# Both feed-forward networks of a hybrid encoder layer in two stages, with seven block products in place of eight for gate and up

## The chip, the core and the metric

The kernel runs on one core of one Trainium2 chip. The metric is the device time of one execution in microseconds (us), lower is better. The core's engines are TensorE (PE; its weight loads are PEld in the profile), VectorE (DVE), ScalarE (ACT), GpSimd (POOL) and SyncE (SP, which issues the DMAs).

## What is computed

One layer of an encoder over 1024 tokens of width 1024, all in float32. It opens and closes with a SwiGLU feed-forward network (FFN) of inner width 2816. Between the two stand a projection, attention, a state-space mixer and a merge, which the change does not touch.

```python
SEQ = D_MODEL = 1024
D_FF = 2816
def _swiglu(x, w_gate, w_up, w_down):
    return (jax.nn.silu(x @ w_gate) * (x @ w_up)) @ w_down
...
        h = h + FFN_RES * _swiglu(_rmsnorm(h, ffn1_norm[l]), ffn1_w_gate[l], ffn1_w_up[l], ffn1_w_down[l])
...
        h = h + FFN_RES * _swiglu(_rmsnorm(h, ffn2_norm[l]), ffn2_w_gate[l], ffn2_w_up[l], ffn2_w_down[l])
    return _rmsnorm(h, final_norm)
```

## The kernel before

`build` runs the phases one after the other with a barrier between them; `ffn_phase` stands first ("f1", rows loaded from x) and last ("f2", with the final norm, class `Finish`). The residual stream lies in SBUF as `rows`, 8 token tiles of 128 x 1024.

**Precision.** Each float32 product is made of three: every operand is split into a high part (ACT rounds it to fp32r, L528) and a low part (DVE or POOL subtracts, L532), and `three_passes` (L46 to L50) issues high x high, high x low and low x high into one PSUM bank. Each matmul has a 128 x 128 stationary and a 128 x 512 moving operand.

**Head.** `Norm` squares the rows (ACT, L283), takes roots, scales (DVE, L325), and PE turns each token tile (8 transposes, L364) into PSUM; ACT and DVE (L339) write it back as `nT_hi` and `nT_lo`. PE starts the first gate product for the first 512 tokens once six of the eight tiles have been turned, and turns the last two between products. POOL splits the low parts of the first four weight tiles (L532).

**Body.** The 2816 inner columns are 11 pairs of 128-wide tiles. For a pair p, `gate_up(p)` makes four products (two tiles, gate and up), each for two halves of the tokens: 8 inner blocks x 3 passes x 2 halves, 192 matmuls in all. ACT applies Silu (L550), DVE multiplies by up (L598), and ACT and DVE split the result into `hT_hi` (L562) and `hT_lo` (L601). `down(q)`, for the pair before, multiplies it by two 128 x 1024 tiles of w_down: 8 token tiles x 2 halves x 2 inner tiles x 3 passes, 96 matmuls. PSUM has eight banks and they are shared: gate, up and down take turns, so after each token tile DVE adds half of the two banks into `rows` (L584, `add`), and the next `gate_up` waits for the last of these adds (`added`). Weights come in pieces of 512 KB through three raw buffers. PE, ACT, DVE and SP loop over pairs, with two pairs in a body (four in number) on PE.

**End.** The last two `down` calls stand back to back. In "f2" the DVE queue mixes the last adds with the scaling of the output rows (L415), and SP stores them.

## Time and profile before

| | us |
|---|---|
| device time, median of 3 runs (2611.12 to 2617.19) | 2611.46 |
| the profiled execution, device time | 2620.58 |
| its span, first to last instruction | 2618.8 |
| PE busy in that span | 2355.1 (90%) |
| DVE / ACT / POOL busy | 1138.8 / 674.0 / 133.8 |
| "f1" and "f2" together | about 60% of the span |

The page cuts the span into 40 slices of 65.5 us. The first 11.8 slices are "f1", the last 12 are "f2"; PE is busy in over 90% of nearly all of them. The profiled execution's own time is 0.35% above the median. PE's busy time is no measure of its rate, since matmuls overlap: the distance between the starts of two of them is.

### The profile page before, as it was taken

To read this page: it belongs to the slowest core of one execution; us is meant where nothing else is said; L and a number is where in the kernel's file an instruction comes from. 1 tells how busy PE (TensorE), PEld (TensorE's weight loads), DVE (VectorE), ACT (ScalarE), POOL (GpSimd) and SP (SyncE) were. 2 spreads that over 40 slices of the span, in tenths; PEclk is the share of its full clock that TensorE was granted. 3 is DMA by queue.
4 is the path that set the end of the run, shared out by engine and by line. 5 is a ranking of instruction groups with operands and counts; after the bars stand their busy time and mean duration, and the time that the engine had idled before them with its cause. 6 is when DMAs were issued, how large, how long until landed. Compare 5 with 4: busy or idle time off the path is not lost. (4 is left out here: it accounts for less than half of the span.)

```text
span 2618.8 us, 27137 instructions
## 1 busy us (share of the span) xinstructions
PE 2355.1 (90%) x10898; PEld 1951.9 (75%) x10898; DVE 1138.8 (43%) x1493; ACT 674.0 (26%) x964; POOL 133.8 (5%) x97
## 2 busy tenths in 40 slices
PE   6999999999978896795968998799799999999997
PEld 5888888888867886685846776577688888888885
DVE  4333333333245294697337777442433333333325
ACT  4211111111112321314226667320321111111112
POOL 1000000000000010220002222000100000000000
PEclk8999999999998998898989999799899999999998
DMA  3211111111012322221240000241221111111101
GB/s 128 81 49 44 45 48 48 48 48 48 16 43 77 88 70 45 57 89 41 81 129 6 6 6 1 86 171 34 71 75 49 49 48 48 42 47 48 48 25 64
DMA packets 174039, 146.96 MB, mean 56 GB/s; under 512 B 27968, under 2 KB 154176, under 8 KB 173952
## 3 DMA queue, kind: packets, MB, share of 16 engines
q1 hardware_dynamic: 173952, 145.77, 18.6%
q8 instruction: 59, 0.97, 0.2%
q14 instruction: 28, 0.23, 0.0%
HBM read 120.58 MB, written 23.07 MB: 55 GB/s over the span
## 5 line engine op out<-in xcount | busy, mean ns | idle before, releaser
L48 PE MATMUL psum<-f_nT_hi,f_w_hi 128*128 128x512 f32 x1408 | 551.7, 392 | 23.9 <-DVE rows L584 23.9
L49 PE MATMUL psum<-f_nT_lo,f_w_hi 128*128 128x512 f32 x1408 | 549.2, 390 | 0.0
L50 PE MATMUL psum<-f_nT_hi,f_w_lo 128*128 128x512 f32 x1408 | 548.7, 390 | 0.0
L48 PEld LDWEIGHTS psum<-f_nT_hi,f_w_hi 128*128 128x128 f32 x1408 | 265.0, 188 | 86.1 <-DVE rows L584 27.8
L584 DVE SCALAR_TENSOR_TENSOR rows<-psum,rows 128x1024 f32<-128x1024 f32 x176 | 215.4, 1224 | 221.2 <-PE psum L50 221.2
L50 PEld LDWEIGHTS psum<-f_nT_hi,f_w_lo 128*128 128x128 f32 x1408 | 264.9, 188 | 55.6
L49 PEld LDWEIGHTS psum<-f_nT_lo,f_w_hi 128*128 128x128 f32 x1408 | 265.0, 188 | 54.4
L48 PE MATMUL psum<-f_d_hi,f_hT_hi 128*128 128x512 f32 x704 | 275.3, 391 | 7.3 <-issue 7.3
L49 PE MATMUL psum<-f_d_lo,f_hT_hi 128*128 128x512 f32 x704 | 275.2, 391 | 0.0
L50 PE MATMUL psum<-f_d_hi,f_hT_lo 128*128 128x512 f32 x704 | 275.1, 391 | 0.0
L532 DVE TENSOR_TENSOR f_w_lo<-f_raw,f_w_hi 128x1024 fp32r<-128x1024 f32 x80 | 97.6, 1220 | 398.3 <-ACT f_w_hi L528 398.3
L598 DVE TENSOR_TENSOR f_xn<-psum,f_xn 128x1024 f32<-128x1024 f32 x44 | 53.9, 1225 | 359.7 <-PE psum L50 359.7
L528 ACT CAST f_w_hi<-f_raw 128x1024 fp32r<-128x1024 f32 x88 | 92.2, 1048 | 333.6 <-PE psum L50 333.6
L48 PEld LDWEIGHTS psum<-f_d_hi,f_hT_hi 128*128 128x128 f32 x704 | 132.8, 189 | 35.8 <-issue 8.0
L50 PEld LDWEIGHTS psum<-f_d_hi,f_hT_lo 128*128 128x128 f32 x704 | 133.0, 189 | 27.7
L49 PEld LDWEIGHTS psum<-f_d_lo,f_hT_hi 128*128 128x128 f32 x704 | 132.9, 189 | 27.8
L550 ACT ACTIVATE f_xn<-psum 128x1024 f32<-128x1024 f32 x44 | 45.2, 1028 | 408.3 <-PE psum L50 408.3
L528 ACT CAST f_d_hi<-f_raw 128x1024 fp32r<-128x1024 f32 x44 | 43.9, 1044 | 388.6 <-PE psum L50 388.6
L1728 DVE TENSOR_TENSOR at_PT_lo<-psum,at_PT_hi 128x512 fp32r<-128x512 f32 x128 | 87.7, 686 | 71.8 <-ACT at_PT_hi L1624 71.5
L48 PE MATMUL psum<-nT_hi,g_hi 128*128 128x512 f32 x256 | 101.8, 398 | 7.2 <-POOL g_lo L164 7.2
L49 PE MATMUL psum<-nT_lo,g_hi 128*128 128x512 f32 x256 | 101.0, 395 | 0.0
L50 PE MATMUL psum<-nT_hi,g_lo 128*128 128x512 f32 x256 | 100.9, 394 | 0.0
(282 smaller groups left out, 3284.6 us busy)
## 6 DMA issues: line engine op xcount, KB each, us to landing
f_raw<-ffn_w_gate SPq DMA_DIRECT2D x44, 512.0 KB, 4.7
f_raw<-ffn_w_up SPq DMA_DIRECT2D x44, 512.0 KB, 3.9
f_raw<-ffn_w_down SPq DMA_DIRECT2D x44, 512.0 KB, 3.5
g_raw<-w_in SPq DMA_DIRECT2D x16, 512.0 KB, 4.7
gates<-rows SPq DMA_DIRECT2D x10, 512.0 KB, 3.0
rows<-x SPq DMA_DIRECT2D x8, 512.0 KB, 7.2
kept<-rows SPq DMA_DIRECT2D x1, 4096.0 KB, 12.9
gl_gate<-gates SPq DMA_DIRECT2D x8, 512.0 KB, 4.6
```

What stands on the lines that cost most here:

```text
L48: pe.matmul(out, lhs_hi, rhs_hi, start=first, stop=False)
L49: pe.matmul(out, lhs_hi, rhs_lo, start=False, stop=False)
L50: return pe.matmul(out, lhs_lo, rhs_hi, start=False, stop=last)
L528: act.copy(dst, raw[slot][:]).then_inc(w_hi_done, 1)
L532: dve.tensor_tensor(dst, raw[slot][:], hi.bitcast(F32), ALU.subtract).then_inc(w_lo_done, 1)
L550: act.activation(two(h[:, t, :]), ps2(2 * t), ACT.Silu).then_inc(silu_done, 1)
L584: dve.scalar_tensor_tensor(out=two(rows[:, m, :]), in0=ps2(m % 4), scalar=0.5, in1=two(rows[:, m, :]), op0=ALU.mult, op1=ALU.add).then_inc ...
L598: dve.tensor_tensor(two(h[:, t, :]), ps2(2 * t + 1), two(h[:, t, :]), ALU.mult).then_inc(mult_done, 1)
L1728: dve.tensor_tensor(pt(PT_lo, g, x), turned_bank(x), pt(PT_hi, g, x).bitcast(F32), ALU.subtract).then_inc(s["tr_lo"], 1)
```

## The change

`ffn_phase` is written anew, for both FFNs. The other phases stay.

**Stage one, gate and up.** For each pair of inner tiles the weight block (1024 x 256) is seen as 2 x 2 blocks A of 512 x 128, and the normed activations (1024 x 1024, turned) as 2 x 2 blocks B of 512 x 512. The product's four quarters come from seven block products in place of eight (Winograd's form of Strassen's scheme), each of 4 inner blocks x 3 passes = 12 matmuls of the same shape as before. Four combinations of B (`T`) are made once in the head by POOL (`combine`), for four pairs of token tiles; PE turns seven 128 x 512 blocks for each pair (`turn`), and ACT and DVE keep the high and low parts of all seven (`B_hi`, `B_lo`). Four combinations of A (`S`) are made by POOL for each of the 22 matrices (11 pairs, gate and up; `sums`). Of a matrix PE makes products q = 0 to 6 into three banks; ACT copies the first (`t1`), and DVE adds `t1`, `t2`, `t3` to the others as they end, which gives the quarters of gate or up in the space of `rows`. The operands of matrix n+1 are split, product by product, while matrix n runs. Silu and gate x up follow, and the hidden activations of the pair go to a DRAM tensor, `hidden`.

**Stage two, down.** All 22 tiles of w_down (512 KB each) are loaded into the space of B as the last matrix frees it. A unit is one inner tile for one half of the tokens: 4 token tiles x 2 halves x 3 passes = 24 matmuls, into all eight banks, which hold the sum over the whole depth of 22 units. There are 44 units; their hidden tiles (256 KB) come back from DRAM through eight buffers. `rows` is loaded again, from x or, in "f2", from a copy in DRAM that is stored in the head. DVE adds a token tile once, at the end of its half. The last adds and the final norm then have their own order.

PE loops over pairs (ten iterations of 168 matmuls) and over units (nine iterations of 48 matmuls for each half); ACT, DVE, POOL and SP are written out without loops.

The diff, cut to its core:

```diff
...
+PAIRS = F // (2 * P)
+MATS = 2 * PAIRS
+FT = F // P
+QUAD = ST // 2
+KH = KT // 2
+PRODUCTS = 7
+GATE_BANKS, UP_BANKS = (7, 0, 1), (2, 3, 4)
+QUARTER = {(0, 0): 0, (1, 1): 1, (1, 0): 2, (0, 1): 3}
...
+        B_hi, B_lo = (at(n, [P, PRODUCTS, KH, HALF], F32R, n) for n in ("B_hi", "B_lo"))
+        A_hi, A_lo = (at(n, [P, PRODUCTS, KH, P], F32R, n) for n in ("A_hi", "A_lo"))
+        raw = [at(f"raw{j}", [P, KT, 2 * P], F32, "raw", 8 * KB * j) for j in range(2)]
...
+        T = at("T", [P, 4, HALF], F32, "raw", 8 * KB)
+        wd_raw = [at(f"wd_raw{k}", [P, D], F32, ("B_hi", "B_lo")[k % 4 // 2], 8 * KB * (k // 4) + 4 * KB * (k % 2)) for k in range(FT)]
+        h_raw = [at(f"h_raw{u}", [P, HALF], F32, "raw", 8 * KB * (u % 2) + 2 * KB * (u // 2)) for u in range(8)]
...
+            load_matrix(0)
+            if x is None:
+                sp.dma_start(residual.rearrange("(m p) d -> p m d", p=P), rows[:]).then_inc(s_kept, 16)
+            sp.wait_ge(s_tr, PRODUCTS * QUAD)
+            load_matrix(1)
+            for p in range(PAIRS):
                 for j in range(2):
...
+                    n = 2 * p + j
+                    if n + 2 < MATS:
+                        sp.wait_ge(s_lo, PRODUCTS * (n + 1))
+                        load_matrix(n + 2)
+                    if j == 0 and p:
+                        sp.wait_ge(s_h, p)
+                        sp.dma_start(hidden[p - 1].rearrange("q f s -> f q s"), h).then_inc(s_hout, 16)
+            def load_unit(u):
+                sh, k = u // FT, u % FT
+                sp.dma_start(h_raw[u % 8][:], hidden[k // 2, QUARTER[k % 2, sh]]).then_inc(s_hraw[u % 8], 16)
+            sp.wait_ge(s_hout, 16 * (PAIRS - 1))
+            sp.wait_ge(s_lo, PRODUCTS * MATS)
+            for u in range(8):
+                load_unit(u)
+            for k in range(FT):
+                if k % 4 == 0:
+                    sp.wait_ge(s_mm, PRODUCTS * (MATS - 1) + k // 4 + 1)
+                sp.dma_start(wd_raw[k][:], w_down[k * P:(k + 1) * P, :]).then_inc(s_wd[k // 4], 16)
+            sp.wait_ge(s_h, PAIRS)
+            sp.dma_start(hidden[PAIRS - 1].rearrange("q f s -> f q s"), h).then_inc(s_hout, 16)
+            sp.wait_ge(s_hout, 16 * PAIRS)
+            sp.wait_ge(s_c12, MATS)
+            for m in range(ST):
+                sp.dma_start(rows[:, m, :], residual[m * P:(m + 1) * P, :]).then_inc(s_res, 16)
...
+            for u in range(8, UNITS):
+                sp.wait_ge(s_dlo, 2 * (u - 7))
+                load_unit(u)
...
+            def matrix(n):
+                p, j = n // 2, n % 2
+                a, b, c = banks[j]
+                if j:
+                    act.wait_ge(s_c12, n)
+                    act.wait_ge(s_g11, p + 1)
+                    act.activation(g[:, 1:4], g[:, 1:4], ACT.Silu).then_inc(s_grest, 1)
+                for q in range(PRODUCTS):
+                    act.wait_ge(s_mm, PRODUCTS * n + q + 1)
+                    if q == 0:
+                        if n:
+                            act.wait_ge(s_t3, n)
+                        elif x is None:
+                            act.wait_ge(s_kept, 16)
+                        act.copy(t1, bank(a)).then_inc(s_t1, 1)
+                    if q == 2 and not j:
+                        if p:
+                            act.wait_ge(s_h11, p)
+                        act.activation(g[:, 0], bank(a), ACT.Silu).then_inc(s_g11, 1)
+                    if n + 1 < MATS:
+                        high(n + 1, q)
...
+            blocks_high(0)
+            blocks_high(1)
+            for q in range(3):
+                high(0, q)
...
+            def unit_high(u):
+                if u >= 2:
+                    act.wait_ge(s_unit, u - 1)
+                elif u == 1:
+                    act.wait_ge(s_mm, PRODUCTS * MATS)
+                else:
+                    act.wait_ge(s_lo, PRODUCTS * MATS)
+                act.wait_ge(s_wd[u % FT // 4], 16 * min(4, FT - u % FT // 4 * 4))
+                act.copy(wd[u % 2][0][:], wd_raw[u % FT][:]).then_inc(s_dhi, 1)
+                act.wait_ge(s_hraw[u % 8], 16 * (u // 8 + 1))
+                act.copy(hh[u % 2][0][:], h_raw[u % 8][:]).then_inc(s_dhi, 1)
...
+            rstd(0)
+            scaled(0)
+            variance(1)
+            rstd(1)
+            scaled(1)
+            variance(2)
+            variance(3)
+            blocks_low(0)
+            rstd(2)
+            scaled(2)
+            blocks_low(1)
+            rstd(3)
+            scaled(3)
+            blocks_low(2)
+            blocks_low(3)
...
+                dst = h if j else g
+                for q in range(PRODUCTS):
+                    dve.wait_ge(s_mm, PRODUCTS * n + q + 1)
+                    if q == 1:
+                        dve.wait_ge(s_t1, n + 1)
+                        dve.tensor_tensor(t2, bank(b), t1, ALU.add).then_inc(s_t2, 1)
+                    if q == 2 and j:
+                        dve.wait_ge(s_g11, p + 1)
+                        if p:
+                            dve.wait_ge(s_hout, 16 * p)
+                        dve.tensor_tensor(h[:, 0], bank(a), g[:, 0], ALU.mult).then_inc(s_h11, 1)
+                    if q == 3:
+                        dve.tensor_tensor(t3, bank(b), t1, ALU.add).then_inc(s_t3, 1)
+                    if q == 4:
+                        dve.wait_ge(s_t3, n + 1)
+                        dve.tensor_tensor(dst[:, 1], bank(c), t3, ALU.add).then_inc(s_c22, 1)
+                    if q == 5:
+                        dve.tensor_tensor(dst[:, 2], bank(b), t3, ALU.add).then_inc(s_c21, 1)
+                    if q == 6:
+                        dve.wait_ge(s_t2, n + 1)
+                        dve.tensor_tensor(dst[:, 3], bank(c), t2, ALU.add).then_inc(s_c12, 1)
+                    if n + 1 < MATS:
+                        low(n + 1, q)
+                if j:
+                    dve.wait_ge(s_grest, p + 1)
+                    dve.wait_ge(s_c12, n + 1)
+                    dve.tensor_tensor(h[:, 1:4], h[:, 1:4], g[:, 1:4], ALU.mult).then_inc(s_h, 1)
...
+            unit_low(0)
+            for u in range(UNITS):
+                if u == FT:
+                    for m in range(QUAD):
+                        add(m)
+                unit_low(u + 1)
...
+                if i:
+                    pool.wait_ge(s_tr, PRODUCTS * i)
+                pool.wait_ge(s_xn, 2 * i + 2)
+                pool.tensor_tensor(T[:, 0], B12, B11, ALU.subtract).then_inc(s_T, 1)
+                pool.tensor_tensor(T[:, 2], B22, B12, ALU.subtract).then_inc(s_T, 1)
+                pool.wait_ge(s_T, 4 * i + 1)
+                pool.tensor_tensor(T[:, 1], B22, T[:, 0], ALU.subtract).then_inc(s_T, 1)
+                pool.wait_ge(s_T, 4 * i + 3)
+                pool.tensor_tensor(T[:, 3], B21, T[:, 1], ALU.subtract).then_inc(s_T, 1)
+            def sums(n):
+                r = raw[n % 2]
+                A11, A21, A12, A22 = r[:, 0:4, 0:P], r[:, 0:4, P:], r[:, 4:8, 0:P], r[:, 4:8, P:]
+                pool.wait_ge(s_raw[n % 2], 16 * (n // 2 + 1))
+                for i, (a, b, op, q) in enumerate(((A21, A22, ALU.add, 4), (S[:, 0], A11, ALU.subtract, 1),
+                                                   (A11, A21, ALU.subtract, 3), (A12, S[:, 1], ALU.subtract, 6))):
+                    if n:
+                        pool.wait_ge(s_lo, PRODUCTS * (n - 1) + q + 1)
+                    if i in (1, 3):
+                        pool.wait_ge(s_sum, 4 * n + (1 if i == 1 else 2))
+                    pool.tensor_tensor(S[:, i], a, b, op).then_inc(s_sum, 1)
+            combine(0)
+            combine(1)
+            sums(0)
+            combine(2)
+            for q in range(3):
+                low_half(pool, 0, q)
+            combine(3)
+            for n in range(1, MATS):
+                sums(n)
...
+            def product(out, q, first, last):
+                for k in range(KH):
+                    mm = three_passes(pe, out, A_hi[:, q, k, :], A_lo[:, q, k, :], B_hi[:, q, k, :], B_lo[:, q, k, :], first and k == 0, last and k == KH - 1, not first)
+                mm.then_inc(s_mm, 1)
...
+            def matrix(p, j, first):
+                n = 2 * p + j
+                a, b, c = banks[j]
+                for q, (out, begin, end) in enumerate(((a, True, True), (b, True, True), (a, False, True), (b, False, True),
+                                                       (c, True, True), (b, True, True), (c, False, True))):
+                    pe.wait_ge(s_lo, n * PRODUCTS + q + 1)
+                    if first and j == 0:
+                        pe.wait_ge(s_blo, PRODUCTS * (QUAD - 1) + q + 1)
+                    if q == 0 and not first:
+                        pe.wait_ge((s_g11, s_h11)[j], p)
+                    if q == 1 and not first:
+                        pe.wait_ge(s_c21, n - 1)
+                    if q == 2:
+                        pe.wait_ge(s_t1, n + 1)
+                    if q == 3:
+                        pe.wait_ge(s_t2, n + 1)
+                    if q == 4 and not first:
+                        pe.wait_ge(s_c12, n - 1)
+                    if q == 5:
+                        pe.wait_ge(s_t3, n + 1)
+                    if q == 6:
+                        pe.wait_ge(s_c22, n + 1)
+                    product(bank(out), q, begin, end)
...
+                pe.wait_ge(s_dlo, u * 2 + 2)
+                for i in range(QUAD):
+                    if first and sh:
+                        pe.wait_ge(s_add, i + 1)
+                    elif first and i == 2:
+                        pe.wait_ge(s_c21, MATS)
+                        pe.wait_ge(s_c12, MATS)
                     for half in range(2):
...
+                        sl = slice(half * HALF, (half + 1) * HALF)
+                        mm = three_passes(pe, tile_banks(i)[:, half, :], hh[par][0][:, i * P:(i + 1) * P], hh[par][1][:, i * P:(i + 1) * P],
+                                          wd[par][0][:, sl], wd[par][1][:, sl], first, final)
+                    if final and i < QUAD - 1:
+                        mm.then_inc(s_tile, 1)
+                mm.then_inc(s_unit, 1)
...
+            for i in range(QUAD):
+                turn(i)
+            for j in range(2):
+                matrix(0, j, True)
+            with pe.Fori(1, PAIRS) as p:
+                for j in range(2):
+                    matrix(p, j, False)
+            for sh in range(2):
+                at = sh * FT
+                unit(at, at % 2, True, False, sh)
+                unit(at + 1, 1, False, False, sh)
+                with pe.Fori(1, FT // 2 - 1) as v:
+                    for par in range(2):
+                        unit(v * 2 + (at + par), par, False, False, sh)
+                unit(at + FT - 2, 0, False, False, sh)
+                unit(at + FT - 1, 1, False, True, sh)
...
```

POOL at the head of "f1", before (all of its work in that FFN; `f_w_lo` is a weight's low part):

```order
L692 UNCONDITIONAL_BRANCH
L621 UNCONDITIONAL_BRANCH [waits barrier_Pool_Activation_PE_DVE_SP_gather]
L532 ISA
L532 TENSOR_TENSOR f_w_lo<-f_raw,f_w_hi 128x1024 [waits f1_w_hi_done] x4
L447 UNCONDITIONAL_BRANCH
```

and now (`f_T` are the combinations of B, `f_S` those of A; the waits named `f1_tr` are for PE's transposes):

```order
L770 TENSOR_TENSOR f_T<-f_xn_A_hi,f_T 128x512 [waits f1_T]
L772 TENSOR_TENSOR f_T<-f_xn_A_hi,f_T 128x512 [waits f1_T]
L767 TENSOR_TENSOR f_T<-f_xn_A_lo 128x512 [waits f1_xn,f1_tr]
L768 TENSOR_TENSOR f_T<-f_xn_A_lo 128x512
L770 TENSOR_TENSOR f_T<-f_xn_A_lo,f_T 128x512 [waits f1_T]
L772 TENSOR_TENSOR f_T<-f_xn_A_lo,f_T 128x512 [waits f1_T]
L784 TENSOR_TENSOR f_S<-f_raw_73 128x512 [waits f1_raw_in0]
L784 TENSOR_TENSOR f_S<-f_S,f_raw_73 128x512 [waits f1_sum]
L784 TENSOR_TENSOR f_S<-f_raw_73 128x512
L784 TENSOR_TENSOR f_S<-f_raw_73,f_S 128x512 [waits f1_sum]
```

POOL has 23 operations of 128 x 512 ahead of the last turned block, in the order combine, combine, sums, combine, three low parts, combine; four operations of 128 x 1024 stood there, on the weights alone.

DVE in the body, before: the last tile of a pair, and two of the eight adds that end it.

```order
L532 TENSOR_TENSOR f_w_lo<-f_raw,f_w_hi 128x1024
L596 REGISTER_ALU
L597 REGISTER_ALU
L598 TENSOR_TENSOR f_xn<-psum,f_xn 128x1024
L531 REGISTER_ALU
L532 TENSOR_TENSOR f_w_lo<-f_raw,f_w_hi 128x1024
L601 TENSOR_TENSOR f_hT_lo<-f_xn,f_hT_hi 128x1024
L583 ISA
L584 SCALAR_TENSOR_TENSOR rows<-psum,rows 128x1024
```

and now, from the second product of an up matrix to the end of its pair (`f1_mm` counts PE's products):

```order
L678 TENSOR_TENSOR rows<-psum,rows 128x512 [waits f1_t1,f1_mm]
L622 TENSOR_TENSOR f_A_lo<-f_S,f_A_hi 128x512 [waits f1_hi]
L683 TENSOR_TENSOR rows<-psum,rows 128x512 [waits f1_hout,f1_g11,f1_mm]
L622 TENSOR_TENSOR f_A_lo<-f_raw_73,f_A_hi 128x512 [waits f1_hi]
L685 TENSOR_TENSOR rows<-psum,rows 128x512 [waits f1_mm]
L622 TENSOR_TENSOR f_A_lo<-f_S,f_A_hi 128x512 [waits f1_hi]
L688 TENSOR_TENSOR rows<-psum,rows 128x512 [waits f1_t3,f1_mm]
L622 TENSOR_TENSOR f_A_lo<-f_S,f_A_hi 128x512 [waits f1_hi]
L690 TENSOR_TENSOR rows<-psum,rows 128x512 [waits f1_mm]
```

The eight adds of a pair (L584) have left the body; a smaller operation on PSUM now follows each product but the first, with the split of the next matrix's operand behind it.

## Rows read from the trace of the kernel before

**Rows 1.** The windows view: busy us (instructions) of each engine, then clock, DMA share, GB/s.
```profile
core 0: us, PE busy (x) PEld busy (x) DVE busy (x) ACT busy (x) POOL busy (x), PEclk, DMA share, GB/s
100.00:200.00 100.00, 98.68 (x435) 81.36 (x434) 33.52 (x28) 16.32 (x16) 0.00 (x0) 1.00 0.16 48
...
750.00:755.00 5.00, 3.95 (x11) 3.13 (x12) 0.95 (x1) 0.00 (x0) 0.00 (x0) 0.71 0.00 0
```

**Rows 2.** The timeline of PE, 75 matmuls apart in one gate_up: start us, us.
```profile
682.66 0.39 PE L48 MATMUL psum<-f_nT_hi,f_w_hi 128*128 128x512 f32 x1
...
699.66 0.39 PE L48 MATMUL psum<-f_nT_hi,f_w_hi 128*128 128x512 f32 x1
```

**Rows 3.** PE's waits in "f1", and the timeline at the first and eighth of nine.
```profile
PE psum L48 <- DVE rows L584: 12.0, 9, 1.4
...
146.34 0.50 PE L48 MATMUL psum<-f_nT_hi,f_w_hi 128*128 128x512 f32 x1 [1.32 <-DVE rows L584]
...
614.87 0.50 PE L48 MATMUL psum<-f_nT_hi,f_w_hi 128*128 128x512 f32 x1 [1.32 <-DVE rows L584]
```

**Rows 4.** The timeline of PE between the last two down calls of "f1".
```profile
747.03 0.39 PE L50 MATMUL psum<-f_d_hi,f_hT_lo 128*128 128x512 f32 x1
751.05 0.47 PE L48 MATMUL psum<-f_d_hi,f_hT_hi 128*128 128x512 f32 x1 [3.63 <-issue]
...
755.43 0.43 PE L48 MATMUL psum<-f_d_hi,f_hT_hi 128*128 128x512 f32 x1
```

**Rows 5.** The head of "f2": ACT's first, PE's first transpose, PE's first product.
```profile
1835.28 1.06 ACT L283 ACTIVATE f_hT_lo<-rows 128x1024 fp32r<-128x1024 f32 x1 [11.74 <-PEq L63]
...
1843.43 3.68 PE L364 MATMUL psum<-ident,f_xn 128*128 128x128 f32 x16 [9.73 <-DVE f_xn L325]
...
1861.88 0.78 PE L48 MATMUL psum<-f_nT_hi,f_w_hi 128*128 128x512 f32 x1
```

**Rows 6.** The timeline of "f1"'s head: DVE's scaling beside POOL's subtractions.
```profile
18.80 1.27 DVE L325 SCALAR_TENSOR_TENSOR f_xn<-rows,f_stat,f_gb 128x1024 f32<-128x1024 f32 x1
...
27.94 2.35 POOL L532 TENSOR_TENSOR f_w_lo<-f_raw,f_w_hi 128x1024 fp32r<-128x1024 f32 x1 [1.89 <-ACT f_w_hi L528]
28.20 3.17 DVE L325 SCALAR_TENSOR_TENSOR f_xn<-rows,f_stat,f_gb 128x1024 f32<-128x1024 f32 x1
...
31.29 1.21 DVE L339 TENSOR_TENSOR f_nT_lo<-psum,f_nT_hi 128x1024 fp32r<-128x1024 f32 x1
```

**Rows 7.** Groups of instructions: busy us, mean ns of one, idle before them.
```profile
L1794 POOL TENSOR_TENSOR at_QT_lo<-at_qf,at_QT_hi 96x512 fp32r<-96x512 f32 x16 | 21.0, 1314 | 34.1 <-ACT at_QT_hi L1617 34.1
...
L1728 DVE TENSOR_TENSOR at_PT_lo<-psum,at_PT_hi 128x512 fp32r<-128x512 f32 x128 | 87.7, 686 | 71.8 <-ACT at_PT_hi L1624 71.5
...
L1624 ACT CAST at_PT_hi<-psum 128x512 fp32r<-128x512 f32 x128 | 71.7, 584 | 28.9 <-PE psum L1546 28.7
...
L231 DVE TENSOR_TENSOR wo_lo<-wo_raw,wo_hi 128x512 fp32r<-128x512 f32 x16 | 11.0, 691 | 66.7 <-ACT wo_hi L221 66.7
...
L598 DVE TENSOR_TENSOR f_xn<-psum,f_xn 128x1024 f32<-128x1024 f32 x44 | 53.9, 1225 | 359.7 <-PE psum L50 359.7
...
L528 ACT CAST f_d_hi<-f_raw 128x1024 fp32r<-128x1024 f32 x44 | 43.9, 1044 | 388.6 <-PE psum L50 388.6
```

**Rows 8.** Transposes of one token tile, cold in the head and warm between products.
```profile
1860.26 1.97 PE L364 MATMUL psum<-ident,f_xn 128*128 128x128 f32 x8 [2.26 <-DVE f_xn L325]
...
39.65 1.04 PE L364 MATMUL psum<-ident,f_xn 128*128 128x128 f32 x8
```

**Rows 9.** The timeline of the end.
```profile
2603.43 0.39 PE L50 MATMUL psum<-f_d_hi,f_hT_lo 128*128 128x512 f32 x1
...
2612.46 2.48 DVE L415 SCALAR_TENSOR_TENSOR f_raw<-rows,f_stat,f_gb 128x1024 f32<-128x1024 f32 x2
```

**Rows 10.** DMA: a busy window, and one issue of 4 MB (KB, us to landing).
```profile
10.00:20.00 10.00, 3.68 (x16) 3.28 (x16) 5.83 (x11) 7.89 (x13) 0.00 (x0) 1.00 1.08 354
...
rows<-kept SPq DMA_DIRECT2D x1, 4096.0 KB, 17.3
```

More of the change, by code:

```diff
@@ L447, in ffn_phase @@
+PAIRS = F // (2 * P)
[6 more added lines that the diff above has]
+QUARTER = {(0, 0): 0, (1, 1): 1, (1, 0): 2, (0, 1): 3}
+def ffn_phase(nc, tag, gain, w_gate, w_up, w_down, rows, ident, psum, hidden, residual, x=None, finish=None):
     with Phase(nc) as ctx:
@@ new lines, in ffn_phase @@
+        s_t1, s_t2, s_t3, s_c22, s_c21, s_c12 = map(sem, ("t1", "t2", "t3", "c22", "c21", "c12"))
+        s_g11, s_grest, s_h11, s_h, s_hout = map(sem, ("g11", "grest", "h11", "h", "hout"))
+        s_wd, s_hraw = [sem(f"wd_in{i}") for i in range(-(-FT // 4))], [sem(f"h_in{i}") for i in range(8)]
+        s_dhi, s_dlo, s_unit, s_tile, s_res, s_add = map(sem, ("dhi", "dlo", "unit", "tile", "res", "add"))
+        last = Rstd(stat, sem("fvar"), sem("fsqrt"), sem("flink"))
+        s_fgain, s_fsq, s_y, s_out = map(sem, ("fgain", "fsq", "y", "out"))
@@ L569, in _, with square @@
-            pair(0, 0, first=True)
-            pair(1, 1)
-            with act.Fori(1, NP // 2) as q:
-                pair(q * 2, 0)
-                pair(q * 2 + 1, 1)
-            pair(NP - 1, (NP - 1) % 2, last=True)
-            if tail:
-                tail.scalar(act)
+            def square(i):
+                for j, m in enumerate(order[i]):
+                    if x is not None:
+                        act.wait_ge(s_x[m], 16)
+                    if i + j:
+                        act.wait_ge(s_sq, 2 * i + j)
+                    act.activation(dump[:], rows[:, m, :], ACT.Square, accum_out=stat[:, 0, 2 * i + j:2 * i + j + 1]).then_inc(s_sq, 1)
@@ new lines, in low @@
+            def low(n, q):
+                low_half(dve, n, q)
+            variance(0)
+            rstd(0)
[13 more added lines that the diff above has]
+            blocks_low(3)
+            for q in range(3, PRODUCTS):
+                low(0, q)
@@ L1933, in build @@
     trig_rows = nc.dram_tensor("trig_rows", [2 * ROPE, SEQ], F32, kind="Internal").ap()
+    hidden = nc.dram_tensor("hidden", [PAIRS, 4, P, HALF], F32, kind="Internal").ap()
     with ExitStack() as ctx:
```

458 lines of the change are left out of this document (204 added, 254 removed).

## The prediction

> **What bounds the kernel now.** I read the page's busy table first (PE 90% of the span), then windows of 100 us: in the body of an FFN PE is busy for 98.7 of 100 us at the full clock of 2.4 GHz, with DVE at 34 and ACT at 16 [rows 1]. Then the timeline of PE, for the rate: 75 matmuls take 699.66 - 682.66 = 17.00 us, 0.2267 us each [rows 2]. An FFN has 11 x (192 + 96) = 3168 matmuls, 718.1 us at that rate, and the stream of "f2" lasts 2603.8 - 1861.9 = 741.9 us from its first product to the end of its last [rows 5, 9]. So the FFNs, 60% of the span, are bound by the number of matmuls. The rest of the 742 is in three places (rows from "f1", which has the same code). (a) At nine boundaries of pairs PE idles 1.32 to 1.41 us for the last add [rows 3]. The period there is (614.87 - 146.34)/7 = 66.93 us against 288 x 0.2267 = 65.28, so the price with the slower restart is 1.65. (b) Between the last two down calls the weights of the second aren't split yet: 13 steps take 755.43 - 747.03 = 8.40 us in place of 2.95 [rows 4]. Of those 5.45 us, 3.8 are idle, and 1.66 are the twelve matmuls from 751.05, which take 4.38 us for 2.72, partly at the lower clock level (granted clock 0.71 in that window [rows 1]). (c) Transposes between the products.
>
> **The change, part by part.** The sum is made against the profiled execution's own 2620.6 us.
>
> *Matmuls.* Gate and up fall from 11 x 192 = 2112 to 22 x 7 x 12 = 1848 for each FFN; down stays at 44 x 24 = 1056. Their shape and their weight loads are the same, so I keep 0.2267. 264 fewer are 59.8 us, for two FFNs **-119.7**. This holds if PE never waits at a product. A product lasts 12 x 0.2267 = 2.72 us. Each wait is for an operation on a bank with one other product in between: `t1` is an ACT copy (0.58 [rows 7]), `t2`, `t3` and `c22` are DVE operations of 128 x 512 on PSUM (0.69 [rows 7]). The longest queue ahead of one is at `t2`: high and low part of the next operand (0.58 + 0.69 [rows 7]) and possibly one POOL operation that blocks DVE (1.31 [rows 7]), most of it before the product ends; `t2` ends 0.8 to 1.5 us after it and has 2.72. Over a matrix of 84 x 0.2267 = 19.0 us DVE has some 10 us of work, ACT 7, POOL 4 x 1.31 = 5.2. The loads (1 MB for a matrix) have 18 us.
>
> *The adds in the body.* With the whole depth in PSUM they are gone, and with them (a): 2 x 9 x 1.65 = **-29.7**. (b) goes too: 2 x 5.45 = **-10.9**. What is late next at that place is the start of stage two. After the last matmul of stage one DVE still makes c12 (0.69), the product of 1536 columns (1.5 x 1.225 = 1.84), the low parts of the first weight (1.22) and hidden tile (0.69) [rows 7]; with hand-offs 4.7 us. A stop of that length cost 1.66 more in slow matmuls [rows 4]. 2 x 6.3 = **+12.6**. Later units have 24 x 0.2267 = 5.44 us, and their preparation takes ACT 1.04 + 0.58 and DVE 1.22 + 0.69, so they are covered. At the change of halves the adds chase the tiles, 1.22 against 1.36 us for a tile: no wait.
>
> *The head.* This is the large debt. Before, PE's first product stands 1861.88 - 1835.28 = 26.6 us after ACT's first operation [rows 5]. Now POOL's queue decides, with 23 operations of 128 x 512 before the last block can be turned. None of that size and kind stands in the FFNs; the nearest row is 1.31 us [rows 7] (half of POOL's 128 x 1024 is 1.2 [rows 6]). I take 1.3: 29.9, and 1 us for waits on the operation before. POOL and DVE exclude each other when DVE reads two operands in SBUF: the scaling at 28.20 lasts 3.17 us, not 1.27, and ends 1.08 after POOL's operation does (27.94 + 2.35), while a DVE operation that reads PSUM at 31.29 keeps its 1.21 [rows 6]. Six scalings fall into POOL's time: 6 x 1.1 = 6.6. The second combine waits for the first turn: 2.1. POOL can start when two tiles have been scaled: PE's first transpose stands at 8.15 after ACT's first [rows 5], plus 1 us because each square now waits for the one before, plus 1.25 for the second tile, 10.4. So POOL ends at 10.4 + 29.9 + 1 + 6.6 + 2.1 = 50.0. The last four-transpose blocks cost 1.97/2 = 0.98 each in the cold state [rows 8]; six of them hang behind the last but one combination, which is ready 1.3 earlier: 50.0 - 1.3 + 5.9 = 54.6. That is 28.0 us later than before, the same in "f1". The two tiles turned in the stream (eight transposes last 1.04 us warm [rows 8], of which 0.8 show) are saved. 2 x (28.0 - 1.6) = **+52.8**. From below: 1.2 an operation and no exclusion give 43.7, 11 us less for each head. From above: DVE's own queue, with 28 low parts of 0.69, waits 1.3 behind POOL at each scaling, and could add 4 us.
>
> *Matrix 1.* Its load shares space with `T` and is issued only at the end of the turns; 1 MB should land 5 to 6 us later, just in time for `t2`'s queue. 0 to 2 us each, **+1** together. The copy of `rows` to DRAM in "f2" has 50 us: nothing.
>
> *The end.* Now 15.1 us follow the last matmul (end 2603.7, span 2618.8), since the DVE mixes adds and rows; the last pair of scalings begins at 2612.46 [rows 9]. In the new order four rows are done long before; after the last matmul stand an add (1.2), a root and five small steps (1.2), two rows (2.5), again 1.5 and two rows (2.5), and the same 3.9 from the end of the scaling to the end: 12.7. **-2.4**.
>
> Sum: -119.7 - 29.7 - 10.9 + 12.6 + 52.8 + 1 - 2.4 = -96.3, so 2524.3 us in the profiled execution. That one is 0.35% above the median, so times 2611.46/2620.58: **2515 us**.
>
> **Rivals.**
>
> *Stage two starves (chance 0.12).* All of w_down is asked for at once: 11.5 MB, then the last hidden store (1 MB), the residual (4.2 MB), and only then hidden tile 8, all in one queue: 17 MB from about 13 us before stage two. At 354 GB/s, the rate of a busy window [rows 10], this takes 48 us, and 4 for store and wait: tile 8 lands at 39, and unit 8 wants it at 4.7 + 8 x 5.44 - 2 = 46. At the rate of the residual's own kind of load, 4.19 MB in 17.3 us or 242 GB/s [rows 10], it lands at 61: a stall of 15 us and 1.7 of slow clock in each FFN, 2515 + 33 = 2548. Against it: that load shared the queues with others.
>
> *Back edges on PE (0.10).* PE now takes (9 + 8 + 8) x 2 = 50 branches back, where it took 6 or so. In the rows of before they lie under the wait for the add: boundaries with a branch and without one both show 1.32 [rows 3], so a branch costs between nothing and 1.32 more than is seen. All of it would be 50 x 1.32 = 66, 2581 us; half a microsecond each gives 2540. I take nothing, since each wait is met one product ahead and PE's queue is full at the branch. The Trainium skill, "Runtime: NRT & Kernel Launch", section Instruction fetch mechanics, speaks against this change: a taken branch whose target lies outside the two pages held forces a fetch before execution goes on. By it the 18 edges over pairs would pay more than those over units. The trace neither confirms nor refutes it, because its stops hide it.
>
> *Slower: PE waits at the products (0.07).* There are 4 x 44 = 176 waits for a bank. Before, the wait for an add with nothing between costs 1.32 [rows 3]; uncovered at each, 176 x 1.32 = 232 us, 2747. The price from which it decides is (96 + 8)/176 = 0.6 us a wait. It would take a queue of over 3.3 us ahead of `t2`, two POOL operations and both splits. For it: DVE, ACT and POOL now have an order of their own around every 2.72 us. Against it: half of DVE's time is free.
>
> *The saving isn't what it says (0.05).* The 5808 matmuls of both FFNs keep their number, but a step of 0.240 in place of 0.2267, by operands in another layout, would give back 77 us: 2592.
>
> **Chances.** Forecast 0.63 (2493 to 2535), starving 0.12, back edges 0.10, slower 0.07, longer step 0.05; 0.03 lies below. A measurement can tell about 0.3% (8 us) from no change. Faster by more 0.91, within 0.03, slower 0.06 (the rivals short of -96 in full stay faster). The range goes from both heads at their lower bound (2515 - 22) to the starved case with a few back edges: 2493 to 2556. It leaves out 0.03 below, most of the slower case and of the longer step, and half of the back edges, some 0.18.
>
> **What the new profile would show.** PE's step of 0.227 in stage one, no idle time ahead of a product, matrices of 19.0 us. PE's first product some 55 us after ACT's first operation, with POOL busy throughout. One stop of 4 to 5 us between the stages; none at unit 8, where hidden tile 8 landed early. No stop at branches (every two units). The end in 12.7 us. I am wrong if PE's idle time in stage one comes before products (the slower rival), if loops show a gap at equal distances, or if the head is decided by DVE or DMA.

## The result, and the profile after

The changed kernel takes 2509.63 us (median of 4 runs, 2508.82 to 2514.70) against 2614.32 us of the kernel before beside it (4 runs, 2611.12 to 2619.70): ratio 0.9602, 95% interval 0.9579 to 0.9625. The forecast was 2515 us. Its profiled execution took 2514.70 us, with a span of 2512.9 against 2618.8, so 105.9 us less where the sum said 96.3. Every difference of spans below compares profiled executions.

The first lines of its page, and the groups of instructions of the two stages (line, engine, operation, shapes, count; then busy us, mean ns of one, and the idle time before them with what ended it):

```profile
span 2512.9 us, 27742 instructions
PE 2251.8 (90%) x10466; PEld 1874.1 (75%) x10466; DVE 1329.5 (53%) x1927; ACT 859.9 (34%) x1360; POOL 437.9 (17%) x303
...
L48 PE MATMUL psum<-f_B_hi,f_A_hi 128*128 128x512 f32 x1232 | 479.7, 389 | 0.2 <-DVE rows L678 0.2
...
L48 PE MATMUL psum<-f_wd_hi,f_hh 128*128 128x512 f32 x704 | 276.0, 392 | 8.8 <-DVE f_hh L709 8.8
...
L622 DVE TENSOR_TENSOR f_A_lo<-f_raw,f_A_hi 128x512 fp32r<-128x512 f32 x128 | 120.7, 943 | 127.2 <-ACT f_A_hi L546 126.7
...
L622 DVE TENSOR_TENSOR f_A_lo<-f_S,f_A_hi 128x512 fp32r<-128x512 f32 x174 | 120.9, 696 | 4.1 <-ACT f_A_hi L546 2.9
```

PE's share is 90% as before, but of a shorter span. In both FFNs together the products wait 0.2 us for a bank, and the down matmuls 8.8: the two stops between the stages. This answers [rows 3] and [rows 4], whose nine waits of 1.3 to 1.4 us and whose 3.8 us are gone. The windows view, for the body of stage one (both FFNs) and the first 50 us of stage two (us, busy us of PE, PEld, DVE, ACT, POOL with their counts, granted clock, DMA share, GB/s), answers [rows 1]:

```profile
60.00:160.00 100.00, 100.00 (x443) 82.78 (x442) 54.52 (x71) 34.36 (x53) 36.59 (x24) 1.00 0.29 94
160.00:260.00 100.00, 100.00 (x443) 82.84 (x442) 54.11 (x69) 29.44 (x47) 32.27 (x20) 1.00 0.25 84
1850.00:1950.00 100.00, 100.00 (x442) 82.80 (x442) 53.56 (x69) 30.90 (x47) 35.11 (x23) 1.00 0.22 74
480.00:490.00 10.00, 7.92 (x28) 6.42 (x29) 3.77 (x5) 1.59 (x3) 0.00 (x0) 0.83 1.03 410
490.00:500.00 10.00, 10.00 (x46) 8.29 (x45) 3.65 (x4) 2.56 (x4) 0.00 (x0) 1.00 0.87 346
...
520.00:530.00 10.00, 10.00 (x45) 8.26 (x45) 3.25 (x4) 3.15 (x4) 0.00 (x0) 1.00 0.18 52
```

PE is busy for 100.00 of 100 us at 2.4 GHz, with DVE at 54 in place of 34 and POOL at 32 to 37 in place of 0. The only window here that isn't full holds the change of stages. DMA falls from 410 GB/s to 52 behind 520, when the weights, the residual and the first hidden tiles have landed.

The timeline: PE's first product and last matmul of the FFNs, the change of stages, and ACT's first operation of "f2". First the kernel before:

```profile
33.05 0.78 PE L48 MATMUL psum<-f_nT_hi,f_w_hi 128*128 128x512 f32 x1
33.62 0.63 PE L49 MATMUL psum<-f_nT_lo,f_w_hi 128*128 128x512 f32 x1
...
774.32 0.39 PE L50 MATMUL psum<-f_d_hi,f_hT_lo 128*128 128x512 f32 x1
```

and the changed one:

```profile
58.32 0.67 PE L48 MATMUL psum<-f_B_hi,f_A_hi 128*128 128x512 f32 x1
58.83 0.40 PE L49 MATMUL psum<-f_B_lo,f_A_hi 128*128 128x512 f32 x1
...
477.31 0.39 PE L50 MATMUL psum<-f_B_hi,f_A_lo 128*128 128x512 f32 x1
482.08 0.80 PE L48 MATMUL psum<-f_wd_hi,f_hh 128*128 128x512 f32 x1 [4.38 <-DVE f_hh L709]
...
485.55 0.40 PE L50 MATMUL psum<-f_wd_hi,f_hh 128*128 128x512 f32 x1
...
722.91 0.39 PE L50 MATMUL psum<-f_wd_hi,f_hh 128*128 128x512 f32 x1
...
1784.06 1.06 ACT L527 ACTIVATE f_dump<-rows 128x1024 f32<-128x1024 f32 x1 [11.74 <-PEq L63]
...
1834.28 0.47 PE L48 MATMUL psum<-f_B_hi,f_A_hi 128*128 128x512 f32 x1
...
2500.12 0.39 PE L50 MATMUL psum<-f_wd_hi,f_hh 128*128 128x512 f32 x1
```

From these rows and [rows 5] the whole difference divides as follows. A stream is counted from an FFN's first product to where its last matmul's step ends.

| part of the span, us | before | after | difference | forecast |
|---|---|---|---|---|
| heads, ACT's first operation to PE's first product, both | 27.3 + 26.6 | 52.9 + 50.2 | +49.2 | +56.0 |
| streams, both | 741.5 + 741.8 | 664.8 + 666.1 | -152.4 | -149.9 |
| between the FFNs, with the first 5 us | 1066.5 | 1066.3 | -0.2 | 0 |
| after the last matmul | 15.1 | 12.55 | -2.5 | -2.4 |
| sum | | | -105.9 | -96.3 |

(The forecast counted the transposes taken out of the stream, 2 x 1.6, with the head; here they stand with the stream.) The same division is used for every experiment below, because the part between the FFNs varies by itself by some 9 us (last section) and a difference of whole spans holds that too.

### The profile page after: what moved, and what is told of

Read it like the earlier page. It is cut to its first block and busy times, and to the rows that moved or that the text cites. A ratio compares the mean times of both kernels' runs of the same rounds, so it can differ in the third digit from the quotient of the medians.

```text
span 2512.9 us, 27742 instructions
## 1 busy us (share of the span) xinstructions
PE 2251.8 (90%) x10466; PEld 1874.1 (75%) x10466; DVE 1329.5 (53%) x1927; ACT 859.9 (34%) x1360; POOL 437.9 (17%) x303
## 5 line engine op out<-in xcount | busy, mean ns | idle before, releaser
L48 PE MATMUL psum<-f_B_hi,f_A_hi 128*128 128x512 f32 x1232 | 479.7, 389 | 0.2 <-DVE rows L678 0.2
L50 PE MATMUL psum<-f_B_hi,f_A_lo 128*128 128x512 f32 x1232 | 479.3, 389 | 0.0
L49 PE MATMUL psum<-f_B_lo,f_A_hi 128*128 128x512 f32 x1232 | 479.3, 389 | 0.0
L48 PE MATMUL psum<-f_wd_hi,f_hh 128*128 128x512 f32 x704 | 276.0, 392 | 8.8 <-DVE f_hh L709 8.8
L49 PE MATMUL psum<-f_wd_lo,f_hh 128*128 128x512 f32 x704 | 275.4, 391 | 0.0
L50 PE MATMUL psum<-f_wd_hi,f_hh 128*128 128x512 f32 x704 | 275.3, 391 | 0.0
L48 PEld LDWEIGHTS psum<-f_B_hi,f_A_hi 128*128 128x128 f32 x1232 | 231.4, 188 | 48.7 <-issue 0.6
L49 PEld LDWEIGHTS psum<-f_B_lo,f_A_hi 128*128 128x128 f32 x1232 | 231.4, 188 | 48.0
L50 PEld LDWEIGHTS psum<-f_B_hi,f_A_lo 128*128 128x128 f32 x1232 | 231.3, 188 | 47.8
L48 PEld LDWEIGHTS psum<-f_wd_hi,f_hh 128*128 128x128 f32 x704 | 133.2, 189 | 37.5 <-DVE f_hh L709 9.6
L49 PEld LDWEIGHTS psum<-f_wd_lo,f_hh 128*128 128x128 f32 x704 | 133.2, 189 | 27.6
L50 PEld LDWEIGHTS psum<-f_wd_hi,f_hh 128*128 128x128 f32 x704 | 133.1, 189 | 27.8
```

Source lines behind the costliest of these rows:

```text
L48: pe.matmul(out, lhs_hi, rhs_hi, start=first, stop=False, skip_group_check=go_on)
L49: pe.matmul(out, lhs_hi, rhs_lo, start=False, stop=False, skip_group_check=go_on)
L50: return pe.matmul(out, lhs_lo, rhs_hi, start=False, stop=last, skip_group_check=go_on)
```

## The experiments

Seven kernels were run. `e1` to `e4` share one set of 10 runs of the kernel before (median 2616.51 us), `e5` to `e7` another of 9 (2613.53 us). Where a run is compared with the changed kernel, the two ratios are subtracted and multiplied by 2614 us; their intervals make such a difference uncertain by some 8 us, so the sizes below rest on the traces.

### e1: the change in "f2" alone

```diff
-        ffn_phase(nc, "f1", ..., rows, ident, psum, hidden, w["x"][0], x=w["x"][0])
+        ffn_phase_old(nc, "f1", ..., rows, ident, psum, x=w["x"][0])
```

> The first FFN as before, the second as changed. Theory (each FFN gains by itself, the middle phases do not move): in the two profiles the first FFN ends and the second starts 51.2 us sooner, and the rest of the span loses 54.7 us; so this kernel is 51 us slower than the changed one and 55 us faster than before, about 2559 us. Rival (part of the gain comes from what one FFN leaves to the phases between, or from DMA traffic of both): the two halves do not add up, by more than 5 us.

Measured: 2563.69 us, ratio 0.9796 (0.9776 to 0.9816). From ACT's first operation of "f2" to the end the trace has 728.2 us, where the kernel before has 783.5 and the changed one 728.8: 55.3 less. PE's waits in "f1" are those of before:

```profile
PE psum L48 <- DVE rows L1017: 12.0, 9, 1.4
```

The other half, 50 us, is that of "f1". Each FFN brings its own, and nothing beyond the spread of the part between them is won or lost there.

### e2: two stages, but eight products

```diff
+                    if q == 6:
+                        for k in range(KH):
+                            three_passes(pe, bank(5), A_hi[:, 6, k, :], ..., k == 0, k == KH - 1)
                     product(bank(out), q, begin, end)
```

Product 6 is made a second time into a bank that nobody reads, so that a matrix has 96 matmuls again. All other engines do the work of the changed kernel.

> The changed kernel, but PE makes product 6 of each matrix a second time into a bank that nobody reads: 96 matmuls a matrix, as many as eight block products have, on the same order of work. Theory (PE is bound by the number of matmuls, step 0.2267 us, waits at products cost nothing): 528 more matmuls are +119.7 us, so about 2629 us, which is 15 us slower than before: the two stages alone lose, all of the gain is the seventh part of the products. Rival (waits at the banks are hidden only partly, an eighth product gives them more time): the step of a matrix grows by less than 12 x 0.2267 = 2.72 us, total below +110.

Measured: 2625.86 us, ratio 1.0038 (1.0025 to 1.0051). Stage one is 59.9 us longer than in the changed kernel in "f1" and 59.4 in "f2", 119.3 together, where 528 x 0.2267 says 119.7. (The spans differ by 119.9, but so close a fit is partly luck: the profiled execution of `e2`, 2634.63 us, is the slowest of its five, and the ratios give 114 with the 8 us of doubt.) The same stop of 4.38 us between the stages stands 59.9 us later:

```profile
542.00 0.80 PE L48 MATMUL psum<-f_wd_hi,f_hh 128*128 128x512 f32 x1 [4.38 <-DVE f_hh L709]
```

So the matmuls left out are worth their full step. And it says what the rest is worth: two stages, the depth in PSUM and the long head, with no saved product, are slower than the kernel before by 9 us (0.4%). Without the product that is left out there is no gain.

I had expected this to mean that the two stages alone lose. It doesn't: `e2` still pays for the combinations in its heads, and these are there for the algebra alone. The table charges the heads with 49.2 us, so the algebra brings about 119.3 - 49.2 = 70 of the 105.9 us, and the two stages some 36. That is an estimate from the table, if a kernel with two stages and eight plain products could keep its heads at 27 us; no such kernel was run.

### e3: the first down unit is prepared early

ACT and DVE split the weight and hidden tile of unit 0 ahead of the last product of stage one, at a place where they have nothing left to prepare:

```diff
                     if n + 1 < MATS:
                         high(n + 1, q)
+                    elif q == 5:
+                        unit_high(0)
...
                     if n + 1 < MATS:
                         low(n + 1, q)
+                    elif q == 5:
+                        unit_low(0)
```

> The changed kernel, but ACT and DVE split the operands of stage two's first unit ahead of the last product of stage one, in place of after it. Theory (the stop between the stages is the splits' queue, and the slow matmuls behind it are its consequence): PE's idle 4.4 us and 1.7 us of slow clock go in each FFN, -12 us, about 2497. Rival (the stop only moves to unit 1, whose operands are still split after the last product: DVE has c12, the product of 1536 columns and two low parts, 4.5 us against 5.44 of unit 0): -6 us or less, with a stop before unit 1.

Measured: 2496.12 us, ratio 0.9546 (0.9526 to 0.9567), about 15 us faster than the changed kernel. The stop in the timeline, and the windows view behind it:

```profile
478.25 0.50 PE L48 MATMUL psum<-f_wd_hi,f_hh 128*128 128x512 f32 x1 [0.52 <-DVE f_hh L679]
```

```profile
478.00:488.00 10.00, 9.75 (x43) 8.07 (x44) 6.12 (x7) 2.96 (x4) 0.00 (x0) 1.00 1.03 409
```

The stop is 0.52 us in place of 4.38, and the granted clock is 1.00 behind it in place of 0.83. The stream of "f1" is 5.4 us shorter and that of "f2" 6.5, 11.9 together where 12 were expected. What is left of the stop and its slow matmuls is 0.8 us in each. That confirms the term (6.3 each) and its cause. (Its span is 18.1 us shorter; 7.2 of these lie between the FFNs, where the code is the same.) There is no new stop at unit 1, which was what could have gone wrong.

### e4: only what the blocks of B need stands in POOL's head

The four sums of matrix 0 and two of the three low parts leave POOL's queue ahead of the last turn. The low parts go to DVE, the sums behind the last combination.

```diff
             combine(1)
-            sums(0)
             combine(2)
-            for q in range(3):
-                low_half(pool, 0, q)
+            low_half(pool, 0, 0)
             combine(3)
-            for n in range(1, MATS):
+            for n in range(MATS):
                 sums(n)
```

> The changed kernel with another order in the head: the four combinations of A for matrix 0 are made by POOL after the last combination of B, and two of the three low parts that POOL makes go to DVE, after the turned blocks. The same work. Theory (the head is a chain of POOL's queue and DVE's scaling, which exclude each other; POOL's operations in the gaps hold DVE's small steps and scalings up by 4 to 5 us before combine 2 and by 3 us before combine 3): PE's first product comes 7 us sooner in each FFN, -14 us, about 2495. Rival A (POOL has room, DVE's own 28 low parts and 8 scalings decide): 0 to -3 us. Rival B (the operands of products 1 and 2 now come too late, and PE waits there for what it gained): a smaller gain with waits ahead of products 1 to 4 of matrix 0.

Measured: 2495.62 us, ratio 0.9541 (0.9527 to 0.9555), about 16 us faster than the changed kernel. The first product stands at 51.03, 7.3 us earlier, and in "f2" 4.7 us sooner after ACT's first:

```profile
51.03 0.53 PE L48 MATMUL psum<-f_B_hi,f_A_hi 128*128 128x512 f32 x1
```

Six operations of 1.27 us less would be 7.6 for each head. The first head gave 7.3, the second only 4.7; why that one gave less was not followed up. Both now last 45.5 to 45.7 us. The two make 12 of the 17 us that its span is shorter; another 3.7 lie between the FFNs, where the code is the same (see the last section). POOL's queue does set the head, and PE doesn't wait in matrix 0 for the operands that are made later.

### e5: the splits go ahead of the bank's operation on DVE

This is the slower rival put to the test: each hand-off on DVE is made later by the split that had stood behind it.

```diff
                 for q in range(PRODUCTS):
                     dve.wait_ge(s_mm, PRODUCTS * n + q + 1)
+                    if n + 1 < MATS:
+                        low(n + 1, q)
                     if q == 1:
...
-                    if n + 1 < MATS:
-                        low(n + 1, q)
```

> The changed kernel, but at every product DVE first splits the next matrix's operand (L622) and only then does its operation on the bank (t2, t3, c22, c21, c12), so that each hand-off is some 1.4 us later, and up to 1.3 more where POOL holds DVE. Theory (a hand-off has 2.72 us of cover; now it ends 2.2 to 3.5 us after its product): most of the 176 waits stay hidden, those that meet a POOL operation show up to 0.8 us each; total +5 to +40 us, and PE's waits name DVE's rows. Rival (the cover is larger than the one product, because POOL seldom meets the splits that precede a bank's operation): 0. The slower rival of the prediction (each hand-off nearly uncovered) would give over +100.

Measured: 2518.05 us, ratio 0.9628 (0.9609 to 0.9648). By the ratios that is 7 us above the changed kernel. In the trace the two streams are 2.7 and 3.3 us longer, 5.9 together; the span is only 1.8 us longer, since 3.9 us less lie between the FFNs. PE's waits on this in "f1" and in "f2", and DVE's timeline in the body (of the kernel `e5`):

```profile
PE psum L48 <- DVE rows L680: 2.7, 1, 2.7
...
PE psum L48 <- DVE rows L680: 3.2, 1, 3.2
```

```profile
203.40 0.69 DVE L622 TENSOR_TENSOR f_A_lo<-f_raw,f_A_hi 128x512 fp32r<-128x512 f32 x1 [1.42 <-ACT f_A_hi L546]
204.01 0.68 DVE L685 TENSOR_TENSOR rows<-psum,rows 128x512 f32<-128x512 f32 x1
```

The bank's operation now stands behind ACT's copy and a split of 0.69 us, and still only one wait in each FFN shows: that of matrix 0, whose split needs the late load of matrix 1 (63.53 in `e5` is ACT's first operation on it). The total lies at the lower end of the +5 to +40 that I had expected, but not for the reason given: stalls where POOL blocks DVE did not come. The body has more room than even this order uses up.

### e6: more data ahead of hidden tile 8

The residual (4.2 MB) is loaded twice; the second copy writes the same values.

```diff
-            for m in range(ST):
-                sp.dma_start(rows[:, m, :], residual[m * P:(m + 1) * P, :]).then_inc(s_res, 16)
+            for again in range(2):
+                if again:
+                    sp.wait_ge(s_res, 16 * ST)
+                for m in range(ST):
+                    sp.dma_start(rows[:, m, :], residual[m * P:(m + 1) * P, :]).then_inc(s_res, 16)
```

> The changed kernel, but SP loads the 4.2 MB of the residual twice, one after the other, between w_down and hidden tile 8. Theory (tile 8 landed some 38 us into stage two and unit 8 wants it at 46): it lands 12 to 14 us later, at about 51, PE stops 4 to 6 us before unit 8 and runs some matmuls slowly behind that: +6 us in each FFN, +12. Rival (there is more room than I counted, since the queue drains faster than 354 GB/s): 0, no stop.

Measured: 2514.23 us, ratio 0.9618 (0.9597 to 0.9640), some 4 us above the changed kernel, though its profiled execution has a span of 2509.6, 3.3 less. In the trace the stream of "f1" is 1.0 us longer and that of "f2" 5.1, and the part between them 8.3 shorter. ACT's timeline in "f1" (the operation that prepares the hidden tile of unit 8), and PE's waits in stage two of "f2":

```profile
526.09 0.62 ACT L602 CAST f_hh<-f_h_raw 128x512 fp32r<-128x512 f32 x1 [2.67 <-DMA f_h_raw<-hidden]
```

```profile
PE psum L48 <- DVE f_hh L712: 7.6, 2, 4.4
```

Tile 8 lands at 526.1 in "f1" and 2298.1 in "f2", against 514.3 and 2292.6 in the changed kernel; counted from the end of stage one it is 12.7 and 12.9 us later, as expected. ACT waits 2.67 us for the tile and PE doesn't in "f1"; in "f2" PE stops for 3.2 us beside the stop of 4.4. What separates the two FFNs is how slowly unit 0 had run before: its 24 matmuls took 2.9 us too long in "f1", which gave the tile more time, and 1.8 in "f2". The expectation of a stop in both FFNs was too dark: one fell away. The mechanism of the rival is real, and 4.2 MB more are just about what it takes.

### e7: e3 and e4 together

> The changed kernel with both edits: the first unit of stage two split ahead of the last product (as in e3), and the combinations of A for matrix 0 and two low parts after the last combination of B (as in e4). Theory (the two touch different places, both on PE's path): they add up, -24 to -28 us on the changed kernel, about 2483 us, 0.950 of before. Rival (they share slack): less than 18 us together.

Measured: 2485.55 us (2483.47 to 2492.35), ratio 0.9507 (0.9488 to 0.9526), about 25 us faster than the changed kernel. PE's only wait in stage two of an FFN is that of `e3`:

```profile
PE psum L48 <- DVE f_hh L678: 0.5, 1, 0.5
```

The two gains add up, since one lies ahead of the stream and the other inside it: in the trace the heads are 11.1 us shorter than the changed kernel's and the streams 11.7, where `e4` gave 12.0 and `e3` 11.9. So the edits are worth some 23 us; the span is 30.8 us shorter because the part between the FFNs is 8.1 shorter in this execution. It beats both kernels.

## Why the prediction was right, point by point

In the spans the sum said -96.3 and -105.9 came. Of the 9.6 us missed, 6.8 are in the heads, 2.5 in the streams and 0.3 elsewhere, all to the same side, so the forecast isn't right because large errors cancelled. Small ones did: the stop between the stages was 0.9 dearer than its term, and inside the heads POOL's start in "f1" (1.7 later) and the longer waits for the first turn (1.1 and 2.1) took back part of what other terms had charged too much.

**Matmuls, -119.7: right.** Stage one of "f1" lasts 482.08 - 4.54 - 58.32 = 419.2 us, where 1848 x 0.2267 is 418.9. `e2` gives the same term by itself (119.3).

**Adds, -29.7, and the last two downs, -10.9: right.** No wait on `rows` is left but one of 0.2 us, and the streams as a whole come out 2.5 us below the sum. No run takes these two terms apart; they rest on the waits that are gone.

**What the sum of the streams missed: 2.5 us.** Before, the products begin at the lower clock level: 0.78 and 0.63 us for the first two, and a granted clock of 0.89 and 0.85 in the first 10 us of the two streams. Now they begin with 0.67 and 0.40, at 0.98 and 1.00:

```profile
1861.90:1871.90 10.00, 10.00 (x44) 8.27 (x43) 6.84 (x4) 2.97 (x3) 2.93 (x2) 0.85 0.45 132
33.00:43.00 10.00, 10.00 (x45) 8.29 (x44) 7.17 (x4) 2.97 (x3) 3.00 (x2) 0.89 0.44 128
```

```profile
58.30:68.30 10.00, 10.00 (x45) 8.28 (x44) 5.99 (x10) 5.13 (x10) 4.08 (x4) 0.98 0.66 210
...
1834.00:1844.00 10.00, 9.78 (x46) 7.85 (x45) 6.02 (x10) 5.03 (x10) 3.50 (x3) 1.00 0.68 212
```

(The first two rows are of the kernel before, the others of the changed one.) The first twelve matmuls, 2.72 us at a full step, took 3.88 and 4.20 us; now they take 3.02 and 2.85. That is 2.2 us. Each of the four token tiles turned in a stream had held up the products by 0.92 us, not 0.8, which is 0.5 more. The stop between the stages costs 0.9 more than its term and matrix 1 costs 0.6 less (both below), and with these four the streams are accounted for. The profile of before showed the slow start, and I had taken it into no term.

**The stop between the stages, 2 x (4.7 + 1.66): right, 0.9 too small.** PE stands for 4.54 us beyond a step in both FFNs. In "f1" the eight matmuls from 482.08 take 3.47 us for 1.81: 1.66 more. In "f2" the slow matmuls cost 2.7, and the granted clock there is lower:

```profile
2258.00:2268.00 10.00, 9.70 (x31) 7.78 (x32) 2.27 (x4) 1.37 (x2) 0.00 (x0) 0.71 1.03 410
```

That is 13.5 us for the 12.6 of the sum. `e3` removes all but 0.8 of each.

**The head: right in its mechanism, too large by 2.4 and 4.4 us.** POOL's timeline in "f1" after, first and last of its 23 operations and its three waits:

```profile
17.46 1.26 POOL L767 TENSOR_TENSOR f_T<-f_xn_A_hi 128x512 f32<-128x512 f32 x1 [15.99 <-DVE f_xn_A_hi L639]
18.69 1.27 POOL L768 TENSOR_TENSOR f_T<-f_xn_A_hi 128x512 f32<-128x512 f32 x1
...
25.77 1.27 POOL L767 TENSOR_TENSOR f_T<-f_xn_A_lo 128x512 f32<-128x512 f32 x1 [3.24 <-PE psum L806]
...
34.62 2.24 POOL L784 TENSOR_TENSOR f_S<-f_raw,f_S 128x512 f32<-128x512 f32 x1
38.09 1.27 POOL L767 TENSOR_TENSOR f_T<-f_xn_A_hi 128x512 f32<-128x512 f32 x1 [1.23 <-DVE f_xn_A_hi L639]
...
49.52 1.27 POOL L767 TENSOR_TENSOR f_T<-f_xn_A_lo 128x512 f32<-128x512 f32 x1 [2.68 <-DVE f_xn_A_lo L639]
...
53.31 1.28 POOL L772 TENSOR_TENSOR f_T<-f_xn_A_lo,f_T 128x512 f32<-128x512 f32 x1
```

| term of the head, us | forecast | "f1" | "f2" |
|---|---|---|---|
| from ACT's first to POOL's first | 10.4 | 12.1 | 9.8 |
| 23 operations, unstretched | 29.9 + 1 | 29.0 | 29.0 |
| exclusion of DVE and POOL | 6.6 | 1.0 + 1.23 + 2.68 | 2.9 + 1.23 |
| wait for the first turn | 2.1 | 3.24 | 4.16 |
| from POOL's end to the first product | 4.6 | 3.7 | 3.1 |
| sum | 54.6 | 52.9 | 50.2 |

(Of the exclusion, the first number is what operations last beyond 1.26, one of 2.24 us in "f1" and three in "f2"; the others are waits for `f_xn`.) Two steps were mis-sized. The operation takes 1.26 us and the next starts at its end; 1.3 and a further 1 us for waits, taken from the nearest row because there was none of its kind, are 1.9 too much. And "six scalings fall into POOL's time: 6 x 1.1" charged POOL for what mostly DVE pays: 22 of POOL's 23 operations in "f1" keep their 1.26 to 1.28 us, while two pairs of scalings take 3.38 and 4.46 us where a pair alone takes 2.48. POOL sees only what of that makes `f_xn` late. The waits for the first turn are 1 to 2 us longer than the forecast. Of the 2.4 us in "f1", the last 0.7 are that its head was already longer before than that of "f2", from which I measured. `e4` confirms that POOL's queue sets the head: six operations less, 7.3 us in "f1".

**Matrix 1, +1: 0.4.** Its load was 5.4 us late (issued at 58.70; ACT's operation on it begins at 64.08), and PE waited 0.2 us, in "f2" only. `e5` shows how near it was: one split ahead of `t2` makes it 2.7 and 3.2.

**The end, 12.7: 12.55.**

**Stage two starves (0.12): did not occur, and its time was right.** Tile 8 is issued at 504.2 and lands 10.0 us later, at 514.3, in "f2" at 2292.6. The sum counted from the last matmul of stage one: from there it is 36.7 and 38.9 us, against the 39 at 354 GB/s. The worse bound, 61 at 242 GB/s, was far off, since the windows of 10 us from 460 to 510 move 304 to 411 GB/s. ACT takes the tile at 523.01, 8.8 us after it landed (7.6 in "f2") and behind its own work, without a wait for DMA:

```profile
522.05 1.05 ACT L597 CAST f_wd_hi<-f_wd_raw 128x1024 fp32r<-128x1024 f32 x1 [3.87 <-PE psum L50]
523.01 0.62 ACT L599 CAST f_hh<-f_h_raw 128x512 fp32r<-128x512 f32 x1
```

PE needs the tile 1.3 us before unit 8 (a split by ACT and one by DVE), which leaves 10 to 12 us of margin. `e6`, with the tile 12.7 to 12.9 us later, uses it up in one FFN and just fits in the other.

**Back edges on PE (0.10): did not occur.** The windows of the changed kernel from 60 to 260 us span four edges over pairs of matrices and show PE busy for 200.00 of 200 us. In 1848 matmuls of stage one 0.3 us are unaccounted for. The Trainium skill, "Runtime: NRT & Kernel Launch", section Instruction fetch mechanics, has a taken branch outside the two held pages wait for a fetch. With 50 edges, over bodies of 168 and 48 matmuls, the trace of this kernel shows no such stall. Whether the targets of these branches lay outside what is held no run shows, so the rule is not refuted by this.

**Slower: waits at the products (0.07): did not occur**, and `e5` shows that it was not near: with every hand-off behind one more operation, two of the 176 waits show.

**A longer step (0.05): did not occur**; 1848 matmuls of stage one take 0.2267 us each, and one with the operands in the new layout lasts 389 ns, where it lasted 390 to 392 before.

## What to carry to other kernels

When PE is the bound at a constant step, a matmul that isn't issued is worth its step, and the price of an algebra that saves some lies in what must be ready before the first one: cost the longest queue of the preparing engines ahead of it, and keep in it only what the first product needs. Between two stages, look for what the second stage's first operand waits for, and move its preparation ahead of the last product of the first. Here the two moves were worth some 23 us together (`e7`), while the body had room to spare (`e5`). And when a change brings two ideas at once, price each by itself: a run without the one (`e2`) still pays for what was added for its sake.
